# Norm factors at the two row changes: rows turned against diag(1/root) instead of normed rows turned against the identity

## What is computed

```
x = x + gt_a * rmsnorm(mix @ w_out, g_post_attn)
h = rmsnorm(x, g_pre_ffn) * (1.0 + sc_f) + sh_f        # first row change
f = (silu(h @ w_gate) * (h @ w_up)) @ w_down
x = x + gt_f * rmsnorm(f, g_post_ffn)
h = rms_norm(x, norm1_w) * (1.0 + scale) + shift       # second row change
proj = h @ w_in + b_in

rmsnorm(x, g) = x * rsqrt(mean(x * x, axis=-1) + 1e-6) * g
```

## Time and profile before

| | before |
|---|---|
| median of three runs | 2265.51 us |
| profiled execution, its own time | 2267.16 us |
| its span in the trace | 2265.4 us |
| TensorE busy | 2229.4 us (98%) |
| VectorE busy | 1814.4 us (80%) |
| ScalarE busy | 1115.7 us (49%) |
| mean granted clock of TensorE | 0.996 |

### The profile page before, as it was taken

The page is one execution under the profiler, slowest core; times in us unless marked ns, Lnnn a source line. Parts: engine busy times, 40 slices in busy tenths (PEclk is TensorE's granted clock), DMA queues, the critical chain, the costliest instruction groups (busy, mean ns, idle before and its releaser), DMA issues.

```text
span 2265.4 us, 26312 instructions
## 1 busy us (share of the span) xinstructions
PE 2229.4 (98%) x10346; PEld 1901.3 (84%) x10346; DVE 1814.4 (80%) x2447; ACT 1115.7 (49%) x1473; POOL 14.7 (1%) x31
## 2 busy tenths in 40 slices
PE   8999999999999999999999999999999999999998
PEld 5378788888888888888878888888888888888887
DVE  6799988988889888987675677998878796565885
ACT  5356677464434444544464444444445544454453
POOL 0000000000000000000000000000000000000000
PEclk9999999999999999999999999999999999999999
DMA  9988889888889888898746665556666657655563
GB/s 402 420 296 325 314 330 340 318 316 299 294 317 333 295 297 297 316 354 333 281 166 217 206 209 200 195 200 214 218 218 218 211 196 276 212 201 201 197 205 129
DMA packets 87758, 598.48 MB, mean 264 GB/s; under 512 B 10145, under 2 KB 10209, under 8 KB 16593
## 3 DMA queue, kind: packets, MB, share of 16 engines
q1 hardware_dynamic: 85538, 588.95, 71.9%
q0 software_dynamic: 1664, 7.19, 1.0%
q10 hardware_dynamic: 432, 0.66, 0.1%
HBM read 594.62 MB, written 2.13 MB: 263 GB/s over the span
## 4 chain that ended last, share of the span: by engine, by line
PE 80%; DVE 12%; DMA 5%; issue 2%; ACT 2%; DVEq 0%; ACTq 0%
PE PS L1188 19%; PE PS L1204 16%; PE PS L1213 16%; PE PS L1205 16%; PE PS L1193 10%; DVE LO L1639 4%; DMA RAW<-in_w_mod 2%; DVE R L1681 2%; DMA RAW<-in_w_first 2%; DVE RAW L1649 2%; ACT HI L676 1%; DVE X L1730 0%; PE PS L1563 0%; DMA RAW<-in_w_ffn 0%; PE PS L1342 0%
## 5 line engine op out<-in xcount | busy, mean ns | idle before, releaser
L676 ACT ACTIVATE HI<-RAW 128x1024 fp32r<-128x1024 f32 x784 | 824.0, 1055 | 987.9 <-PE PS L1213 604.1
L1639 DVE TENSOR_TENSOR LO<-RAW,HI 128x1024 fp32r<-128x1024 f32 x784 | 955.8, 1223 | 368.5 <-ACT HI L676 364.4
L1204 PE MATMUL PS<-HI,XH 128*128 128x512 f32 x2080 | 800.2, 385 | 4.0 <-ACT HI L676 2.9
L1205 PE MATMUL PS<-HI,XL 128*128 128x512 f32 x2080 | 789.0, 379 | 0.0
L1213 PE MATMUL PS<-LO,XH 128*128 128x512 f32 x2080 | 535.8, 379 | 2.7 <-DVE LO L1639 2.6
L1204 PEld LDWEIGHTS PS<-HI,XH 128*128 128x128 f32 x2080 | 393.7, 189 | 63.3 <-DVE XL L1911 4.1
L1213 PEld LDWEIGHTS PS<-LO,XH 128*128 128x128 f32 x2080 | 392.8, 189 | 59.8 <-DVE LO L1639 4.1
L1205 PEld LDWEIGHTS PS<-HI,XL 128*128 128x128 f32 x2080 | 393.7, 189 | 53.7
L1188 PE MATMUL PS<-HI,XH 128*128 128x512 f32 x1056 | 315.6, 381 | 1.9 <-DVE XL L1753 1.3
L1188 PE MATMUL PS<-HI,XL 128*128 128x512 f32 x1056 | 314.5, 379 | 0.0
L1193 PE MATMUL PS<-LO,XH 128*128 128x512 f32 x1056 | 273.2, 380 | 0.0
(11 more groups left out here) (263 smaller groups left out, 876.5 us busy)
## 6 DMA issues: line engine op xcount, KB each, us to landing
RAW<-in_w_second SPq DMA_DIRECT2D x208, 1024.0 KB, 4.9
RAW<-in_w_mod SPq DMA_DIRECT2D x144, 1024.0 KB, 5.9
RAW<-in_w_ffn SPq DMA_DIRECT2D x88, 1024.0 KB, 4.9
RAW<-in_w_first SPq DMA_DIRECT2D x64, 1024.0 KB, 5.9
RAW<-in_w_down SPq DMA_DIRECT2D x44, 1024.0 KB, 5.6
BIAS<-in_b_in SPq DMA_DIRECT2D x40, 256.0 KB, 5.2
R<-mod_rows POOLq DMA_DIRECT2D x3, 1024.0 KB, 9.0
X<-in_x SPq DMA_DIRECT2D x2, 1024.0 KB, 9.0
```

Of the source, the lines that this page charges most:

```text
L676: act.activation(HI[:, (it["half"] + hf) % HLS, :], whole, ACT.Copy).then_inc(s.hi_ready, 1)
L1204: pe.matmul(PS[:, bank + u, :], XH[:, 2 * n + kk, rows], hi, start=start and kk == 0, stop=False)
L1205: pe.matmul(PS[:, bank + u, :], XL[:, 2 * n + kk, rows], hi, start=False, stop=False)
L1639: dve.tensor_tensor(LO[:, slot, :], RAW[:, it["slot"], hf * 1024:(hf + 1) * 1024], HI[:, slot, :].bitcast(F32), ALU.subtract).then_inc(s.l ...
```

## The change

At both row changes XN and `normed_rows` go. VectorE instead multiplies the identity by RSTD, one 128x128 instruction for each tile of rows and change (`diagonal`), and TensorE's turn of a block becomes an ordinary float32 product of the block of X, as it is, with that diagonal. The turned and normed block comes out at the same place. The waits on `rows_normed` now ask for the diagonal of the tile alone.

```diff
--- before.py
+++ after.py
@@ -453,6 +453,7 @@
         ROT = region(14336, 2, 512)
         JUNKW = region(14336, 2, 512)
         PX = region(15360, 4, 256)
+        DIAG = [region(at, NT, P) for at in (15360, 10240)]
         PT = region(16384, 8, 384)
         MASKA = region(19456, 384)
         MASKB = region(19840, 384)
@@ -1267,15 +1268,15 @@
                 at = (k % 2) * S + u * P
                 return pe.transpose(PS[:, k // 2, at:at + P], XN[:, u, k * P:(k + 1) * P], IDENT[:])
 
-            def turn_pair(t, n, us, rows):
-
-                pe.wait_ge(s.rows_normed, rows)
+            def turn_pair(t, n, us):
+
+                pe.wait_ge(s.rows_normed, 2 + 2 * t + us[-1])
                 if n >= 4:
                     pe.wait_ge(s.pair_out, turn_no(t, n - 4, 1))
                 for kk in range(2):
                     for i, u in enumerate(us):
-                        m = pe.transpose(turned_to(t, n, us)[:, kk, i * P:(i + 1) * P], XN[:, u, (2 * n + kk) * P:(2 * n + kk + 1) * P],
-                                         IDENT[:])
+                        m = pe.matmul(turned_to(t, n, us)[:, kk, i * P:(i + 1) * P], X[:, u, (2 * n + kk) * P:(2 * n + kk + 1) * P],
+                                      DIAG[t][:, u, :], start=True, stop=True, skip_group_check=True)
                 m.then_inc(s.pair_t, 1)
 
             def keep_busy(bank, count):
@@ -1494,16 +1495,16 @@
                     m.then_inc(s.half_used, 1)
 
             keep_busy(7, 16)
-            turn_pair(0, 0, (0,), 2)
+            turn_pair(0, 0, (0,))
             keep_busy(7, 16)
             pe.wait_ge(s.wo_out, 5)
             for h in range(2):
                 first_half_of_ffn(h, 0)
-            turn_pair(0, 0, (1,), 3)
-            turn_pair(0, 1, (0, 1), 4)
+            turn_pair(0, 0, (1,))
+            turn_pair(0, 1, (0, 1))
             for h in range(2):
                 first_half_of_ffn(h, 1)
-            turn_pair(0, 2, (0, 1), 5)
+            turn_pair(0, 2, (0, 1))
 
             sec = secs["ffn"]
             for it in sec.items:
@@ -1522,7 +1523,7 @@
                     products(sec.half(0, h) + 1, h % HLS, k + hf, lambda u, cc: 4 * q + 2 * u + cc, k + hf == 0, k + hf == NK - 1)\
                         .then_inc(s.half_used, 1)
                     if h in (3, 5, 7, 9, 11):
-                        turn_pair(0, (h + 3) // 2, (0, 1), 5 + (h > 3))
+                        turn_pair(0, (h + 3) // 2, (0, 1))
             pe.wait_ge(s.f_ready, 10)
             down_products()
 
@@ -1572,7 +1573,7 @@
 
             def beside(h):
                 if h < 5:
-                    turn_pair(1, 3 + h, (0, 1), 10)
+                    turn_pair(1, 3 + h, (0, 1))
                 if 8 <= h < 16:
                     gate_columns(h - 8)
                 if h == 26:
@@ -1591,21 +1592,21 @@
             pe.wait_ge(s.sq_done, 8)
             keep_busy(0, 24)
             for n in range(2):
-                turn_pair(1, n, (0,), 7)
+                turn_pair(1, n, (0,))
             keep_busy(0, 16)
             for h in range(2):
                 pe.wait_ge(s.x_ready, PARTS_BEFORE + turn_no(1, h, 0))
                 narrow_high(sec, h, h, bank_of(0), h == 0, (0,))
             narrow_low(sec, 0, 0, bank_of(0), False, (0,))
             for n in range(2):
-                turn_pair(1, n, (1,), 8)
+                turn_pair(1, n, (1,))
             keep_busy(7, 4)
             narrow_low(sec, 1, 1, bank_of(0), False, (0,))
-            turn_pair(1, 2, (0, 1), 9)
+            turn_pair(1, 2, (0, 1))
             for h in range(2):
                 pe.wait_ge(s.x_ready, PARTS_BEFORE + turn_no(1, h, 1))
                 narrow(sec, h, h, bank_of(0), h == 0, False, (1,))
-                turn_pair(1, 3 + h, (0, 1), 9 + h)
+                turn_pair(1, 3 + h, (0, 1))
 
             for h in range(2, HALVES_2):
                 g, n = divmod(h, 8)
@@ -1719,10 +1720,8 @@
                 dve.wait_ge(s.root_ready, no)
                 link(dve.reciprocal(RSTD[:, u:u + 1], ROOT[:, u:u + 1]))
 
-            def normed_rows(us, cols):
-                for u in us:
-                    m = dve.tensor_scalar(XN[:, u, cols], X[:, u, cols], RSTD[:, u:u + 1], None, ALU.mult)
-                m.then_inc(s.rows_normed, 1)
+            def diagonal(t, u):
+                dve.tensor_scalar(DIAG[t][:, u, :], IDENT[:], RSTD[:, u:u + 1], None, ALU.mult).then_inc(s.rows_normed, 1)
 
             def residual_piece(src, u, n):
 
@@ -1768,7 +1767,7 @@
                 dve.wait_ge(s.sq_done, 4)
                 mean_square(0, SQP[:, 0, :])
                 rstd(0, ROOT_ROWS[0][0])
-                normed_rows((0,), slice(0, 256))
+                diagonal(0, 0)
                 dve.wait_ge(s.wo_sq, 8)
                 mean_square(1, SQG[:, 1, :])
                 out_gain(3, 3, 1)
@@ -1781,13 +1780,10 @@
                 dve.wait_ge(s.sq_done, 6)
                 mean_square(1, SQP[:, 1, :])
                 rstd(1, ROOT_ROWS[0][1])
-                normed_rows((1,), slice(0, 256))
-                normed_rows(range(NT), slice(256, 512))
+                diagonal(0, 1)
                 turned_low(0, 0, (1,))
-                normed_rows(range(NT), slice(512, 1024))
                 turned_low(0, 1, (0, 1))
                 first_split(secs["ffn"], 2)
-                normed_rows(range(NT), slice(1024, 2048))
                 first_split(secs["ffn"], 3)
                 turned_low(0, 2, (0, 1))
 
@@ -1811,7 +1807,7 @@
                 dve.wait_ge(s.sq_done, 9)
                 mean_square(0, SQP[:, 0, :])
                 rstd(0, ROOT_ROWS[1][0])
-                normed_rows((0,), slice(0, 512))
+                diagonal(1, 0)
                 dve.wait_ge(s.sq_done, 10)
                 out_part(1, 1)
                 dve.wait_ge(s.sq_done, 11)
@@ -1827,12 +1823,10 @@
                 dve.wait_ge(s.sq_done, 13)
                 mean_square(1, SQP[:, 1, :])
                 rstd(1, ROOT_ROWS[1][1])
-                normed_rows((1,), slice(0, 512))
+                diagonal(1, 1)
                 first_split(secs["second"], 1)
-                normed_rows(range(NT), slice(512, 1024))
                 turned_low(1, 0, (1,))
                 turned_low(1, 1, (1,))
-                normed_rows(range(NT), slice(1024, 2048))
                 turned_low(1, 2, (0, 1))
                 first_split(secs["second"], 2)
                 turned_low(1, 3, (0, 1))
```

## The result

Over 17 runs each the changed kernel has a median of 2271.35 us, the kernel before 2266.58. The two medians differ by 4.8 us. The ratio of the runs is 1.0019, which is 4.3 us, with a 95% interval of 1.0013 to 1.0026: slower by 2.9 to 5.9 us, 0.19%. The forecast was +4.1 us, 0.18%. The median of the kernel before itself came out 1.07 us above that of its first three runs.

What follows compares the result with a forecast made beforehand. TensorE, busy 98% of the span, was taken to bound the kernel. The first change's +2.1 us and the second's +2.0 us gave +4.1 us on the median of 2265.51, so 2269.6 us, range 2266.7 to 2271.3.

Steps and rivals of the forecast that it cites:

- rival 6: The clock falls at the second change too: +5.6 us, 2271.1 us; chance 0.04.
- The pair in the stream: In TensorE's full stream a pair of four blocks goes from 0.44 to 0.88 us as products: +0.44 us.
- The diagonal: On VectorE each of four diagonals takes 0.22 us, from a 128x128 tensor_scalar row; the normings' slope would give 0.28.
- the start of the second change: Second change, half 0 of tile 1 starts at 1155.66 in place of 1155.90: -0.24 us, bounds -0.5 and +0.2.
- The start of the first change: First change, XL of pair 0 and the product at 455.57 come 0.2 us later.
- The waits for XL given back: First change, TensorE's waits of 0.24 and 0.50 us near 477 and 483 go, 0.74 us together; XL slips 0.64.
- The clock: Behind the first change the clock falls to 1.2 GHz, costing 1.47 us; with the change it may hold.
- Rivals 1: Forecast itself: clock as in the median run on both sides, +4.1 us, 2269.6 us; chance 0.46.
- rival 2: The clock fell in the median run before and holds now: +2.6 us, 2268.1 us; chance 0.25.
- a dear product: A product costs four turns in the stream at both changes: +14.8 us, 2280.3 us; chance 0.04.
- a slipping loop: First change, XL's loop slips as far as TensorE and the waits stay: +4.85 us, 2270.4 us; chance 0.12.
- rival 5: VectorE's freed 6.4 us shorten TensorE's waits at both changes, half of them gone: +1.3 us, 2266.8 us; chance 0.09.

Runs made afterwards that it cites:

- e2_second: Kernel before with diagonals and products at the second row change only, the first as before; median 2269.41 us, ratio 1.0013 to the kernel before.
- e7_turn2_first: Kernel before with the turns of pairs 2 to 7 at the first change issued twice, norming on VectorE as before; ratio 1.0010 over 11 runs.
- e8_free: Changed kernel with blocks of X turned with the identity in place of the product with the diagonal, norming left out; ratio 0.9999 over 11 runs.
- e1_first: Changed kernel with the second row change as before, so diagonals and products at the first only; median 2268.93 us, ratio 1.0010 to the kernel before.
- e6_filled: Kernel before with 20 busy turns put into TensorE's holes at both changes; 2266.24 us against 2266.94, ratio 0.9997.
- e10_order_filled: Kernel before with 20 busy turns in TensorE's holes and LO of half 3 moved ahead of the last normings; 2266.01 us against 2266.50, ratio 0.9998.

## Why the prediction was right, point by point

**The sum.** For the same clock the change costs 691.05 - 689.40 = 1.65 us in A and 44.18 - 41.97 = 2.21 in B, 3.9 us together; the forecast had 2.1 and 2.0. The whole runs say 4.3 (2.9 to 5.9), the medians 4.8. The absolute median, 2271.35, lies 0.05 us above the top of the range, 2271.3, since the kernel before was itself slower by 1.07 than the median that the range was built on; the difference is inside it. The ends of the range are not quite the sums that are named for them. The lower bounds with the clock held give 1.6 + 1.7 - 1.5 = +1.8 and so 2267.3 in place of 2266.7, both upper bounds give +5.3 and so 2270.8, and rival 6 gives 2271.1. The line of 4.5 us for a difference that can be told from none was too high as well: over 17 runs each the interval is 1.5 us to either side. So the difference is told from none, where I gave 0.65 to one that is not; by the line itself, 0.2%, it falls just short of slower.

**The pair in the stream, +0.44.** Right: 0.81 against 0.36 us to the next product, +0.45, and 0.224 against 0.108 for one block. L1393 was the row to go by.

**The diagonal, 0.22.** Too low: 0.29. Of the two ends I took the nearer form, a multiply by fixed numbers, and the other end, the slope of the normings, was right. In the kernel before, a norming of 256 columns whose factor is one value a row takes 0.35 where a multiply with fixed numbers takes 0.29 at the same size (L2009), and the same surcharge was due here. It moved the start of the second change: -0.06 us (1155.90 to 1157.53, less the 1.69 by which the changed kernel was late at 1136.93) in place of -0.24. Two diagonals at 0.07 make 0.14 of the 0.18.

**The start of the first change, +0.2.** Right: 455.57 to 456.90 is 1.33, less the 1.12 by which that execution was late at the reciprocal, 0.21.

**The waits for XL given back, 0.74.** The direction was right and the size holds for the fallen clock alone; with the clock held they are 1.2 us, and all of it is given back. The step that failed is the reason: I wrote that VectorE's relief is worth nothing behind the point where TensorE is full, because VectorE already waits for ScalarE there, and that XL slips by 0.64 us. With the clock held VectorE doesn't wait there: in e2_second it has no hole from 457.58 to 473.65. And XL doesn't slip by that much, for the load behind LO of half 3 goes out 461.32 - 453.84 = 7.48 us behind the reciprocal in place of 8.60. XL of pair 3 starts 17.00 us behind the reciprocal in the changed kernel against 16.92 in e2_second, XL of pair 4 at 22.09 against 22.74, XL of pair 5 at 28.49 against 28.88. TensorE's lateness is enough by itself (e7_turn2_first), the relief nearly so (e8_free). For the sum it made no difference; it would have, had the products been cheaper. The 0.45 us by which A came out below the forecast is the size of this term, 1.2 in place of 0.74; that B came out 0.2 above it brings the total nearer, which is luck.

**The clock.** Rivals 1, 2 and 6 differ by the executions they assume, and the profiles show that the fall comes and goes in one and the same piece of code: B of the changed form held in the changed kernel and fell in e2_second, and B of the old form held in the kernel before and fell in e1_first. Between the two profiled executions rival 2 is what happened, in A: 0.57 + 2.21 = 2.8 us for the two stretches, where it had 2.6. Over many runs a mean of both states is measured. That the change makes the clock hold in A is neither shown nor ruled out: it held in all executions with the changed form and in all but one with the old one. The Trainium skill (TensorE: Matmul & The Clock Gate, Part 4: PE-mode transpose) says that transposes don't count as busy for the clock in the way that products do. By that rule a first change made of turns should have lost the clock more readily, and turns in the holes should not help; the traces don't bear it out, since the clock stayed at 2.4 GHz in A in e2_second and in both stretches in e6_filled and e10_order_filled. That is three executions, and with turns at the same place it also fell once.

**The rivals of a dear product and of a slipping loop.** Both out: 2.1 turns to a product, and no wait for XL behind the start.

**The rival of VectorE's relief (rival 5).** Its mechanism is real and its size too large: with products at the price of turns, e8_free, the stretches shorten by 1.2 + 0.5 = 1.7 us, not 3.5, and with the products' true price little of it is left: in A TensorE's lateness swallows the same waits, and in B the products ahead of tile 1's start take 0.43 of the 0.5.

## What to carry to other kernels

Folding a scale into a transpose makes it an ordinary float32 product, which stands as two records where the transpose stands as one and takes 2.1 times as long. It is nearly free only where TensorE stands idle, and each one in a full stream is paid in whole. Relief of an engine that is off the critical path is to be followed through what it frees, here a slot for a load, before it is written down as nothing. Where whole runs scatter by more than the effect, cut the trace at marks ahead of and behind the edit, and compare only executions with the same granted clock. Where a wait inside the stretch hangs on a load, one execution is good to some tenths of a microsecond and no better.

## What the runs showed of the hardware

The fall of TensorE's clock at a row change is a matter of the single execution. At the same place of the same code it is there or not, and its price depends on what lies in it: 0.44 and 0.48 us at the second change with turns, 1.14 with products, and 1.1 at the first, where waits that grow in its absence give back a part of its 1.47. A further scatter of some microseconds lies ahead of the first change, where the reciprocal of tile 0 comes between 444.44 and 447.92 us in the profiled executions of code that is the same up to there. The load of 1 MB that is awaited ahead of pair 4's scaling took 5.1 to 5.9 us from its issue until ScalarE had it where the load ahead of it went out 7.2 to 7.5 us behind the reciprocal, and 6.4 to 7.2 us where that one went out 8.6 to 8.8 us behind it.
